# Nine raw weight buffers in the expert units, and six more for each small unit's first round

## The chip, the cores and the metric

One core of one Trainium2 chip runs the whole program. The metric is the device time of one execution in microseconds (us). Engines: PE (TensorE, matmuls), PEld (its weight loads), DVE (VectorE), ACT (ScalarE), POOL (GpSimd) and SP (SyncE, which here only issues DMAs).

## What is computed

A decoder trunk of two layers on 272 tokens (16 learned meta tokens and 256 real ones) of width 1024. Layer 0: stick-breaking attention and a dense SwiGLU. Layer 1: differential attention and a top-2-of-8 mixture of experts. The change touches the mixture alone:

```
logits = x @ w_router;  top_v, top_i = top_k(logits, 2);  gates = softmax(top_v)
for e in range(8):
    out += combine[:, e] * ((silu(x @ w_gate[e]) * (x @ w_up[e])) @ w_down[e])
```

Everything is float32. An expert has three matrices of 1024 x 3584 (gate, up, and down turned round), together 44 MB; all eight are read from the chip's memory once, 352 MB in 336 pieces.

## The kernel before

**Units.** The experts are taken as eight units, in the order wide, wide, small, wide, small, wide, small, wide. A wide unit holds up to 128 tokens, a small one up to 64; the experts are sorted by their number of tokens so that they fit. More wide units can follow if the tokens are spread unevenly.

**Pieces.** A unit's weights come as PIECES = 42 pieces of 128 x 2048 float32 (1 MB). For each of FC = 7 groups of 512 hidden columns there are two pieces of gate, two of up and two of down. Piece 0 is the first. SP issues one DMA per piece, in order, into one of RAW_SLOTS = 7 raw buffers (six quarters of `raw` and one `raw_more`), piece p into buffer p mod 7.

**A wide unit** multiplies in split form, to keep float32 precision at TensorE's faster rate: ACT copies a piece to `wh` (high half, line 880), DVE subtracts to get `wl` (low half, line 1427), and PE multiplies high x high, high x low and low x high (lines 2235, 2236, 2241 for gate and up, 2259, 2260, 2267 for down). `wh` and `wl` each have SPLIT_SLOTS = 3 places of a piece. A raw buffer is free when DVE has made the low half (`wl_ready`). A place of `wh` or `wl` is free when PE has read it (`wh_used`, `w_used`).

**A small unit** multiplies the raw float32 pieces directly, gate and up side by side in the two column halves of the array (lines 2360, 2362), down likewise in two halves (line 2391). It uses neither `wh` nor `wl`. A raw buffer is free when PE has multiplied with it (`few_used`, which rises by 2 after a pair of gate and up pieces).

**What SP waits for.** Before piece p SP waits until the piece 7 places earlier in the stream has freed its buffer: in a wide unit `wl_ready`, in a small one `few_used`, and for the first seven of a unit the count of the unit before. SP's waits are in order: while it waits for one buffer it issues nothing behind. The loop over the three pairs (small unit, wide unit) is a `Fori`; it reads each unit's expert number with a `value_load` ahead of each of its two units.

**Around it.** At the end of a wide unit ACT copies the 128 x 1024 output to `y`, and POOL stores it (512 KB, line 617) and then fetches the rows of the unit after the next (line 609); their DMAs run on POOL's queue, through the same 16 DMA engines.

Of the kernel before, what the change touches and what calls it, by code (L numbers as in the profile page):

```python
# [27 lines left out]
F32R = mybir.dt.float32r  # L28
# [6 lines left out]
P = 128  # L35
# [10 lines left out]
E = 8  # L46
# [6 lines left out]
CHUNK = 4096  # L53
# [40 lines left out]

RAW_SLOTS, SPLIT_SLOTS = 7, 3
MAX_UNITS = E + 4
# [87 lines left out]
def build(nc, tokens, vectors, sb_qkv, sb_o, d_qkv, d_o, ffn_gate, ffn_up, ffn_down, router, moe_gate, moe_up, moe_down, final_norm,  # L184
          c_base, c_stick, c_diff, c_route, c_zero, out):
    ctx = ExitStack()
    with ctx:
# [9 lines left out]
        raw = sb("raw", [P, 3, CHUNK])  # L197
        wh = sb("wh", [P, 2, CHUNK], F32R)
        wl = sb("wl", [P, 2, CHUNK], F32R)

        hT = sb("hT", [P, KD, L])
# [63 lines left out]
        def experts(own):  # L265
# [12 lines left out]
            return b  # L278

        xh, xl = phase(parts)  # L280
        sq3, raw_more = phase(lambda own: (sb("sq3", [P, 4 * BANK], where=own), sb("raw_more", [P, PIECE], where=own)))
# [10 lines left out]
        raw_landed = [sem(f"raw_landed{i}") for i in range(3)]  # L292
        piece_landed = [sem(f"piece_landed{i}") for i in range(RAW_SLOTS)]
        wh_ready, wl_ready = sem("wh_ready"), sem("wl_ready")
# [91 lines left out]
        for i in range(FC):  # L386
            for half in range(2):
                few_pieces[few_up_at(i) + 2 * half] = ("g", i, half)
                few_pieces[few_up_at(i) + 2 * half + 1] = ("u", i, half)
                few_pieces[few_down_at(i) + half] = ("d", i, half)  # L390

        def raw_piece(p):

            slot = p % RAW_SLOTS
            if slot == RAW_SLOTS - 1:
                return raw_more[:]
            return raw[:, slot // 2, slot % 2 * PIECE:(slot % 2 + 1) * PIECE]

# [8 lines left out]

        def piece_in(u, p):

            return u * (16 * PIECES // RAW_SLOTS) + 16 * (p // RAW_SLOTS + 1)  # L410

# [30 lines left out]
        def _(sp):  # L442
# [25 lines left out]

            def load_piece(e, p, kind, i, half):

                source = weights_of[kind][bass.ds(e * (FC * 2 * P) + P * (2 * i + half), P), :]
                sp.dma_start(raw_piece(p), source).then_inc(piece_landed[p % RAW_SLOTS], 16)

            def load_first():
                for p in range(PIECES):
                    kind, i = unit_chunks[p // 2]
                    if p < RAW_SLOTS:

                        sp.wait_ge(wl_ready, max(c for c in range(C_MOE) if c % 3 == min(p // 2, 2)) + 1 if p < 6 else C_MOE)
                    else:  # L480
                        sp.wait_ge(wl_ready, C_MOE + p + 1 - RAW_SLOTS)
                    load_piece(0, p, kind, i, p % 2)

            def load_wide(a, e, few_before):

                for p in range(PIECES):
                    kind, i = unit_chunks[p // 2]
                    if few_before is not None and p < RAW_SLOTS:
                        sp.wait_ge(few_used, few_before * PIECES + PIECES + p + 1 - RAW_SLOTS)
                    else:  # L490
                        sp.wait_ge(wl_ready, a * PIECES + C_MOE + p + 1 - RAW_SLOTS)
                    load_piece(e, p, kind, i, p % 2)

            def load_few(v, e):

                for p, (kind, i, half) in enumerate(few_pieces):
                    if p < RAW_SLOTS:
                        sp.wait_ge(wl_ready, (v + 1) * PIECES + C_MOE + p + 1 - RAW_SLOTS)
                    else:
                        sp.wait_ge(few_used, v * PIECES + p + 1 - RAW_SLOTS)  # L500
                    load_piece(e, p, kind, i, half)

            load_first()
            sp.wait_ge(routed, 1)
            load_wide(1, sp.value_load(bm["unit_i"][0:1, 1:2], min_val=0, max_val=E - 1), None)
            with sp.Fori(1, len(SMALL_UNITS) + 1) as v:
                load_few(v, sp.value_load(bm["unit_i"][0:1, bass.ds(2 * v, 1)], min_val=0, max_val=E - 1))
                load_wide(v + 1, sp.value_load(bm["unit_i"][0:1, bass.ds(2 * v + 1, 1)], min_val=0, max_val=E - 1), v)

            wides = sp.value_load(bm["unit_i"][0:1, 15:16], min_val=WIDE_UNITS, max_val=MAX_UNITS - len(SMALL_UNITS))  # L510
            with sp.If(wides > WIDE_UNITS):
                with sp.Fori(WIDE_UNITS, wides) as a:
                    e = sp.value_load(bm["unit_i"][0:1, bass.ds(a + len(SMALL_UNITS), 1)], min_val=0, max_val=E - 1)
                    load_wide(a, e, None)

# [114 lines left out]
        def _(act):  # L630
# [242 lines left out]

            def unit_split(u, a, p, first=False):

                act.wait_ge(piece_landed[p % RAW_SLOTS], piece_in(u, p))

                act.wait_ge(wh_used, split_free(a, p, first))
                act.wait_ge(wl_ready, split_free(a, p, first))
                act.copy(split_piece(wh, p), raw_piece(p)).then_inc(wh_ready, 1)  # L880
# [89 lines left out]

            def unit_body(u, a, scatter, first=False, few_next=False):

# [5 lines left out]
                for j, (kind, i) in enumerate(unit_chunks):  # L978
                    if 2 * j + 3 < PIECES:
                        unit_split(u, a, 2 * j + 3)  # L980
                    if kind == "d" and i + 1 < FC:
                        turned_high(i + 1)
                    if 2 * j + 4 < PIECES:
                        unit_split(u, a, 2 * j + 4)
                    if (kind, i) == ("g", 1):
# [20 lines left out]

            unit_body(0, 0, False, first=True)
            unit_split(1, 1, 0)
            unit_split(1, 1, 1)
            output_out(1, 1)  # L1010
            unit_split(1, 1, 2)
            with act.Fori(1, len(SMALL_UNITS) + 1) as v:
                unit_body(2 * v - 1, v, False, few_next=True)
                output_out(2 * v, v + 1)
                few_body(v)
                unit_split(2 * v + 1, v + 1, 0)
                unit_split(2 * v + 1, v + 1, 1)
                few_out(v)
                unit_split(2 * v + 1, v + 1, 2)

# [10 lines left out]
            wides = act.value_load(bm["unit_i"][0:1, 15:16], min_val=WIDE_UNITS, max_val=MAX_UNITS - len(SMALL_UNITS))  # L1031
            unit_body(STORED, WIDE_UNITS - 1, True)
            with act.If(wides > WIDE_UNITS):
                for n in range(2 * QT):
                    scale_for_more(n)
                with act.Fori(WIDE_UNITS, wides) as a:
                    u = a + len(SMALL_UNITS)
                    last_outputs(u, a)
                    unit_split(u, a, 0)
                    unit_split(u, a, 1)  # L1040
                    unit_split(u, a, 2)
                    gathered_high(a + 1)
                    unit_body(u, a, True)

# [671 lines left out]
        def _(pe):  # L1716
# [628 lines left out]
            def few_body(v):  # L2345

                def up(i, half):

                    p = few_up_at(i) + 2 * half
                    out_, few = ps[:, i % 2, :], bm["few"]  # L2350
                    pe.wait_ge(piece_landed[p % RAW_SLOTS], piece_in(2 * v, p))
                    pe.wait_ge(piece_landed[(p + 1) % RAW_SLOTS], piece_in(2 * v, p + 1))
                    if half == 0 and i >= 2:

                        pe.wait_ge(few_prod, (v - 1) * FC + i - 1)
                    for k in range(KD // 2):
                        to = slice((half * (KD // 2) + k) * SMALL, (half * (KD // 2) + k + 1) * SMALL)
                        s = slice(k * WIDE, (k + 1) * WIDE)
                        first_, last_ = half == 0 and k == 0, half == 1 and k == KD // 2 - 1
                        g = pe.matmul(out_[0:SMALL, :], few[:, to], raw_piece(p)[:, s], start=first_, stop=last_,  # L2360
                                      skip_group_check=True)
                        u = pe.matmul(out_[SMALL:, :], few[:, to], raw_piece(p + 1)[:, s], start=first_, stop=last_,  # L2362
                                      skip_group_check=True)
                    g.then_inc(few_used, 1)
                    u.then_inc(few_used, 1)
# [11 lines left out]
                def down(i, half):  # L2377

                    p = few_down_at(i) + half
                    if half == 0:  # L2380
                        pe.wait_ge(few_act_ready, (v - 1) * FC + i + 1)
                        if i == 0:

                            pe.wait_ge(y_ev, 4 * v + 2)
                    pe.wait_ge(piece_landed[p % RAW_SLOTS], piece_in(2 * v, p))
                    for k in range(2):
                        to = slice((half * 2 + k) * SMALL, (half * 2 + k + 1) * SMALL)
                        first_, last_ = i == 0 and half == 0 and k == 0, i == FC - 1 and half == 1 and k == 1
                        for h in range(2):
                            s = slice(k * D + h * BANK, k * D + (h + 1) * BANK)  # L2390
                            ins = pe.matmul(ps[h * SMALL:(h + 1) * SMALL, 2, :], bm["few_act"][:, i % 2, to], raw_piece(p)[:, s],
                                            start=first_, stop=last_, skip_group_check=True)
# [93 lines left out]
```

## Time and profile before

| | us |
|---|---|
| median of 3 runs (1406.06 to 1407.02) | 1406.73 |
| the profiled execution | 1405.3 |
| its span | 1403.5 |

| engine | busy us | share |
|---|---|---|
| PE | 1325.2 | 94% |
| DVE | 875.6 | 62% |
| ACT | 724.1 | 52% |
| POOL | 69.6 | 5% |
| SP's DMA queue | 422.67 MB | 76.4% of 16 DMA engines' time |

The busy share is an average over stages. A matmul counts as busy also while it is stretched or waits inside the engine, so a high share doesn't mean that PE does all it can. The mixture of experts fills the last two thirds of the span. The granted clock of TensorE was 0.985 of its full speed on average.

### The profile page before, as it was taken

To read this page: it belongs to the slowest core of one execution; us is meant where nothing else is said; L and a number is where in the kernel's file an instruction comes from. 1 tells how busy PE (TensorE), PEld (TensorE's weight loads), DVE (VectorE), ACT (ScalarE), POOL (GpSimd) and SP (SyncE) were. 2 spreads that over 40 slices of the span, in tenths; PEclk is the share of its full clock that TensorE was granted. 3 is DMA by queue.
4 is the path that set the end of the run, shared out by engine and by line. 5 is a ranking of instruction groups with operands and counts; after the bars stand their busy time and mean duration, and the time that the engine had idled before them with its cause. 6 is when DMAs were issued, how large, how long until landed. Compare 5 with 4: busy or idle time off the path is not lost.

```text
span 1403.5 us, 19596 instructions
## 1 busy us (share of the span) xinstructions
PE 1325.2 (94%) x7528; PEld 1031.4 (73%) x7528; DVE 875.6 (62%) x954; ACT 724.1 (52%) x719; POOL 69.6 (5%) x92
## 2 busy tenths in 40 slices
PE   9999999999999999999997889998779998888997
PEld 8999999999999778888852258872238884226786
DVE  6554766544987699988830168860128881017897
ACT  7564544344566777777720057750027771006775
POOL 0100000000000063000000000000000000002000
PEclk9999999999999999999999999999999999999999
DMA  8563553553442799999989999989999999999992
GB/s 315 194 224 120 180 180 121 193 183 108 175 166 69 276 343 380 421 407 406 372 317 421 421 407 421 416 339 387 421 420 407 421 359 356 421 421 420 421 421 105
DMA packets 75877, 440.55 MB, mean 314 GB/s; under 512 B 7296, under 2 KB 9344, under 8 KB 30672
## 3 DMA queue, kind: packets, MB, share of 16 engines
q1 hardware_dynamic: 71680, 422.67, 76.4%
q0 software_dynamic: 3952, 16.49, 3.3%
q8 instruction: 66, 1.08, 0.3%
q14 instruction: 35, 0.29, 0.1%
q10 hardware_dynamic: 144, 0.02, 0.0%
HBM read 433.12 MB, written 11.01 MB: 316 GB/s over the span
## 4 chain that ended last, share of the span: by engine, by line
PE 72%; DMA 13%; DVE 7%; issue 4%; ACT 3%; SPq 0%; DVEq 0%; ACTq 0%
PE ps L2235 9%; PE ps L2236 9%; PE ps L2241 8%; DMA raw<-in_moe_w_gate 8%; PE ps L2360 7%; PE ps L1740 4%; PE ps L2259 4%; PE ps L2267 4%; PE ps L2260 4%; PE ps L1730 4%; PE ps L1731 4%; DMA raw<-in_moe_w_up 3%; PE ps L1778 2%; PE ps L1795 2%; PE ps L1779 2%
## 5 line engine op out<-in xcount | busy, mean ns | idle before, releaser
L1427 DVE TENSOR_TENSOR wl<-raw,wh 128x2048 fp32r<-128x2048 f32 x180 | 410.9, 2290 | 62.5 <-ACT wh L880 61.5
L880 ACT CAST wh<-raw 128x2048 fp32r<-128x2048 f32 x180 | 344.3, 1914 | 144.7 <-PE ps L2236 57.2
L2235 PE MATMUL ps<-wh,gh 128*128 128x512 f32 x560 | 222.0, 396 | 11.5 <-issue 8.4
L2236 PE MATMUL ps<-wh,gl 128*128 128x512 f32 x560 | 220.6, 394 | 0.0
L2360 PE MATMUL ps<-raw,few 128*64 128x512 f32 x288 | 139.3, 633 | 37.1 <-issue 28.7
L2362 PE MATMUL ps<-raw,few 128*64 128x512 f32 x312 | 155.8, 650 | 0.0
L2241 PE MATMUL ps<-wl,gh 128*128 128x512 f32 x560 | 151.3, 392 | 0.2 <-DVE wl L1427 0.2
L944 ACT ACTIVATE sil<-ps 64x512 f32<-64x512 f32 x21 | 12.4, 588 | 261.6 <-PE ps L2362 261.6
L2235 PEld LDWEIGHTS ps<-wh,gh 128*128 128x128 f32 x560 | 106.2, 190 | 37.3 <-issue 13.5
L2360 PEld LDWEIGHTS ps<-raw,few 128*64 128x64 f32 x288 | 39.2, 145 | 120.0 <-issue 120.0
L2236 PEld LDWEIGHTS ps<-wh,gl 128*128 128x128 f32 x560 | 106.2, 190 | 23.0
L2241 PEld LDWEIGHTS ps<-wl,gh 128*128 128x128 f32 x560 | 105.3, 188 | 23.9 <-DVE wl L1427 0.7
L1091 DVE TENSOR_TENSOR wl<-raw,wh 128x4096 fp32r<-128x4096 f32 (+1 forms) x18 | 73.2, 4069 | 61.8 <-ACT wh L639 39.7
L639 ACT CAST wh<-raw 128x4096 fp32r<-128x4096 f32 (+2 forms) x29 | 92.0, 3174 | 34.9 <-PE ps L1731 34.3
L2259 PE MATMUL ps<-wh,eah 128*128 128x512 f32 x272 | 109.2, 401 | 0.0
L1618 DVE COPY few_act<-ps 128x256 f32<-128x256 f32 x21 | 8.9, 425 | 159.6 <-PE ps L2374 159.6
L2260 PE MATMUL ps<-wh,eal 128*128 128x512 f32 x272 | 106.5, 391 | 0.0
L1730 PE MATMUL ps<-xh,wh 128*128 128x272 f32 x352 | 88.5, 288 | 0.2 <-DVE xl L1098 0.2
L1731 PE MATMUL ps<-xl,wh 128*128 128x272 f32 x352 | 88.3, 286 | 0.0
L1614 DVE TENSOR_TENSOR act<-sil,ps 64x512 f32<-64x512 f32 x21 | 14.5, 691 | 108.4 <-ACT sil L944 108.4
L2267 PE MATMUL ps<-wl,eah 128*128 128x512 f32 x272 | 73.4, 392 | 0.0
L1427 DVE TENSOR_TENSOR wl<-raw_more,wh 128x2048 fp32r<-128x2048 f32 x30 | 68.6, 2288 | 4.7 <-ACT wh L880 4.6
(353 smaller groups left out, 2378.2 us busy)
## 6 DMA issues: line engine op xcount, KB each, us to landing
raw<-in_moe_w_gate SPq DMA_DIRECT2D x101, 1024.0 KB, 11.3
raw<-in_moe_w_up SPq DMA_DIRECT2D x99, 1024.0 KB, 10.6
raw<-in_moe_w_down SPq DMA_DIRECT2D x88, 1024.0 KB, 12.1
raw_more<-in_moe_w_down SPq DMA_DIRECT2D x24, 1024.0 KB, 10.7
raw_more<-in_moe_w_up SPq DMA_DIRECT2D x13, 1024.0 KB, 14.1
raw<-in_diff_w_qkv SPq DMA_DIRECT2D x8, 1536.0 KB, 6.1
raw_more<-in_moe_w_gate SPq DMA_DIRECT2D x11, 1024.0 KB, 7.3
raw<-in_sb_w_qkv SPq DMA_DIRECT2D x7, 1536.0 KB, 7.7
```

The lines of the kernel that those rows point to most:

```text
L880: act.copy(split_piece(wh, p), raw_piece(p)).then_inc(wh_ready, 1)
L1427: dve.tensor_tensor(split_piece(wl, p), raw_piece(p), raw_f(split_piece(wh, p)), ALU.subtract).then_inc(wl_ready, 1)
L1730: pe.matmul(outp(m), w, highs(k), start=first and k == 0, stop=False, skip_group_check=True)
L1731: ins = pe.matmul(outp(m), w, lows(k), start=False, stop=False, skip_group_check=True)
L2235: pe.matmul(ps[:, bank, :], gh[:, s], w, start=(k0 + k == 0), stop=False)
L2236: ins = pe.matmul(ps[:, bank, :], gl[:, s], w, start=False, stop=False)
L2241: ins = pe.matmul(ps[:, bank, :], gh[:, s], low[:, k * WIDE:(k + 1) * WIDE], start=False, stop=(k0 + k == KD - 1))
L2259: pe.matmul(ps[:, 2 + h, :], ah[:, s], w, start=(i == 0 and k0 + k == 0), stop=False)
L2260: ins = pe.matmul(ps[:, 2 + h, :], al[:, s], w, start=False, stop=False)
L2267: ins = pe.matmul(ps[:, 2 + h, :], ah[:, s], w, start=False, stop=(i == FC - 1 and k0 + k == 3))
L2360: g = pe.matmul(out_[0:SMALL, :], few[:, to], raw_piece(p)[:, s], start=first_, stop=last_, skip_group_check=True)
L2362: u = pe.matmul(out_[SMALL:, :], few[:, to], raw_piece(p + 1)[:, s], start=first_, stop=last_, skip_group_check=True)
```

## The change

There are now RAW_SLOTS = 9 raw buffers for all expert units. The two new ones are the fourth quarters of `wh` and `wl`, which three split places leave unused in the expert stage. Beside them a small unit has LENT = 6 further buffers in its first round: the three places of `wh` and the three of `wl`, which the wide unit before it leaves as it ends.

The modulo rule gives way to two tables. WIDE_PLACES takes 42 pieces in rounds of 9, 8, 9, 8 and 8, so that each unit uses each buffer a fixed number of times; piece 41 of a wide unit follows piece 33 in its buffer instead of piece 34, and pieces 0 to 7 of a small unit follow pieces 34 to 41 of the wide one (before, pieces 0 to 6 followed 35 to 41). Piece 8 of a small unit goes where piece 25 was. FEW_PLACES takes the small unit's pieces in rounds of 15, 9, 9 and 9. Pieces 9 to 14 wait until PE has read pieces 39, 40 and 41 of the wide unit in high form (`wh_used`) or in low form (`w_used`). Piece 15 waits for piece 0, and from there on each waits for the one 9 earlier in its round.

At the very start of the mixture, pieces 7 and 8 of the first unit wait for the end of the attention's output projection (`w_used` at C_MOE) instead of for the first two low halves.

In SP's loop both `value_load`s now stand ahead of the small unit's loads. The counts that ACT and PE wait for are written with two factors (wide units and small units so far) instead of one. Multiplications, splits and all other work stay as they are. The core of the diff:

```diff
-RAW_SLOTS, SPLIT_SLOTS = 7, 3
+RAW_SLOTS, SPLIT_SLOTS = 9, 3
+LENT = 2 * SPLIT_SLOTS
+
+def places(rounds):
+    return [(s, n) for n, r in enumerate(rounds) for s in r]
+
+WIDE_PLACES = places((range(9), range(8), range(9), range(8), range(8)))
+FEW_PLACES = places((range(RAW_SLOTS + LENT), range(9), range(9), range(9)))
...
+        def raw_place(s):
+            if s < 6:
+                return raw[:, s // 2, s % 2 * PIECE:(s % 2 + 1) * PIECE]
+            if s == 6:
+                return raw_more[:]
+            part_, slot = (s - 7, SPLIT_SLOTS) if s < RAW_SLOTS else ((s - RAW_SLOTS) % 2, (s - RAW_SLOTS) // 2)
+            return unsplit[:, part_, slot // 2, slot % 2 * PIECE:(slot % 2 + 1) * PIECE]
...
+        def landed_by(a, few, taken, p):
+            s = taken[p][0]
+            wide_times, few_times = (sum(1 for at_ in t if at_[0] == s) for t in (WIDE_PLACES, FEW_PLACES))
+            return 16 * (wide_times * a + few_times * few + sum(1 for at_ in taken[:p + 1] if at_[0] == s))
...
+            def load_wide(a, e, few=None, first=False):
+                for p, (s, n) in enumerate(WIDE_PLACES):
+                    kind, i = unit_chunks[p // 2]
+                    if n:
+                        sp.wait_ge(wl_ready, a * PIECES + C_MOE + last_at(WIDE_PLACES[:p], s) + 1)
+                    elif first and s < 6:
+                        sp.wait_ge(wl_ready, max(c for c in range(C_MOE) if c % 3 == min(p // 2, 2)) + 1)
+                    elif first:
+                        sp.wait_ge(wl_ready if s == 6 else w_used, C_MOE)
+                    elif few is None:
+                        sp.wait_ge(wl_ready, a * PIECES + C_MOE - PIECES + last_at(WIDE_PLACES, s) + 1)
                     else:
+                        sp.wait_ge(few_used, few * PIECES + last_at(FEW_PLACES, s) + 1)
+                    load_piece(e, raw_piece(p), s, kind, i, p % 2)
+
+            def load_few(v, e):
+                for p, (kind, i, half) in enumerate(few_pieces):
+                    s, n = FEW_PLACES[p]
+                    if n:
+                        sp.wait_ge(few_used, v * PIECES + last_at(FEW_PLACES[:p], s) + 1)
+                    elif s < RAW_SLOTS:
+                        sp.wait_ge(wl_ready, v * PIECES + C_MOE + last_at(WIDE_PLACES, s) + 1)
                     else:
+                        lent = s - RAW_SLOTS
+                        sp.wait_ge((wh_used, w_used)[lent % 2], (v + 1) * PIECES + C_MOE + lent // 2 + 1 - SPLIT_SLOTS)
+                    load_piece(e, few_piece(p), s, kind, i, half)
...
             with sp.Fori(1, len(SMALL_UNITS) + 1) as v:
-                load_few(v, sp.value_load(bm["unit_i"][0:1, bass.ds(2 * v, 1)], min_val=0, max_val=E - 1))
-                load_wide(v + 1, sp.value_load(bm["unit_i"][0:1, bass.ds(2 * v + 1, 1)], min_val=0, max_val=E - 1), v)
+                few_e = sp.value_load(bm["unit_i"][0:1, bass.ds(2 * v, 1)], min_val=0, max_val=E - 1)
+                next_e = sp.value_load(bm["unit_i"][0:1, bass.ds(2 * v + 1, 1)], min_val=0, max_val=E - 1)
+                load_few(v, few_e)
+                load_wide(v + 1, next_e, few=v)
```

## Rows read from the trace of the kernel before

**Rows 1.** The page's second part: moved GB/s in 40 slices of the span.
```profile
GB/s 315 194 224 120 180 180 121 193 183 108 175 166 69 276 343 380 421 407 406 372 317 421 421 407 421 416 339 387 421 420 407 421 359 356 421 421 420 421 421 105
```

**Rows 2.** Windows: us, busy per engine, then granted clock, DMA share, GB/s.
```profile
590.00:697.00 107.00, 107.00 (x484) 87.97 (x483) 95.19 (x56) 80.61 (x55) 2.74 (x5) 1.00 1.01 399
...
717.00:722.00 5.00, 5.00 (x25) 1.91 (x25) 0.00 (x0) 1.07 (x2) 0.57 (x1) 1.00 0.45 181
722.00:727.00 5.00, 5.00 (x26) 1.65 (x24) 0.69 (x1) 0.59 (x1) 2.18 (x4) 1.00 0.91 314
727.00:740.00 13.00, 9.21 (x44) 2.75 (x40) 1.12 (x2) 0.59 (x1) 0.00 (x0) 1.00 1.01 350
740.00:816.00 76.00, 62.73 (x270) 22.00 (x272) 8.61 (x15) 4.01 (x7) 0.00 (x0) 0.93 1.01 421
```

**Rows 3.** Timeline of SP, the DMA issues at the first small unit's start.
```profile
713.83 0.33 SPq L472 DMA_DIRECT2D raw_more<-in_moe_w_gate  x1
721.54 0.33 SPq L472 DMA_DIRECT2D raw<-in_moe_w_up  x1
```

**Rows 4.** DMA issues in short windows at three unit changes; last column: us to landing.
```profile
raw_more<-in_moe_w_gate SPq DMA_DIRECT2D x1, 1024.0 KB, 4.9
raw<-in_moe_w_up SPq DMA_DIRECT2D x1, 1024.0 KB, 5.8
...
raw<-in_moe_w_gate SPq DMA_DIRECT2D x1, 1024.0 KB, 4.7
raw<-in_moe_w_up SPq DMA_DIRECT2D x1, 1024.0 KB, 5.0
...
raw<-in_moe_w_gate SPq DMA_DIRECT2D x1, 1024.0 KB, 4.9
raw<-in_moe_w_up SPq DMA_DIRECT2D x1, 1024.0 KB, 5.7
```

**Rows 5.** Chain of waits, 715 to 860: start us, us, what.
```profile
750.16 3.46 PE ps L2391 x16
753.79 15.20 DMA raw<-in_moe_w_gate
...
808.08 10.68 DMA raw<-in_moe_w_gate
818.91 1.91 ACT wh L880
```

**Rows 6.** Timeline of SP at the two later small units' starts and one end.
```profile
918.06 0.33 SPq L472 DMA_DIRECT2D raw_more<-in_moe_w_down  x1
925.09 0.34 SPq L472 DMA_DIRECT2D raw<-in_moe_w_gate  x1
925.63 0.33 SPq L472 DMA_DIRECT2D raw<-in_moe_w_up  x1
...
946.62 0.33 SPq L472 DMA_DIRECT2D raw<-in_moe_w_up  x1
...
1031.44 0.33 SPq L472 DMA_DIRECT2D raw_more<-in_moe_w_down  x1
1032.75 0.34 SPq L472 DMA_DIRECT2D raw<-in_moe_w_gate  x1
...
1149.74 0.34 SPq L472 DMA_DIRECT2D raw<-in_moe_w_gate  x1
...
1171.50 0.33 SPq L472 DMA_DIRECT2D raw<-in_moe_w_up  x1
```

**Rows 7.** Timeline of DVE, two low halves near the second small unit.
```profile
912.94 2.29 DVE L1427 TENSOR_TENSOR wl<-raw,wh 128x2048 fp32r<-128x2048 f32 x1 [0.45 <-ACT wh L880]
915.75 2.29 DVE L1427 TENSOR_TENSOR wl<-raw_more,wh 128x2048 fp32r<-128x2048 f32 x1
```

**Rows 8.** Timeline of POOL at the first small unit's start.
```profile
719.34 0.57 POOL L617 DMA_DIRECT2D output_slots<-y  x1 [107.64 <-ACT y L953]
```

**Rows 9.** Windows: one whole period, small unit and wide unit.
```profile
717.90:942.90 225.00, 203.79 (x897) 126.72 (x896) 114.75 (x76) 94.27 (x70) 5.98 (x11) 0.97 0.98 397
```

More of the change, by code:

```diff
@@ L278, in experts, with splits @@
             return b
+        def splits(own):
+            return sb("wh", [P, 2, CHUNK], F32R, where=own), sb("wl", [P, 2, CHUNK], F32R, where=own)
+        wh, wl = phase(splits)
+        unsplit = phase(lambda own: sb("unsplit", [P, 2, 2, CHUNK], where=own))
+        sb("splits", [P, 4 * CHUNK])
         xh, xl = phase(parts)
@@ L292, in build @@
         raw_landed = [sem(f"raw_landed{i}") for i in range(3)]
-        piece_landed = [sem(f"piece_landed{i}") for i in range(RAW_SLOTS)]
+        piece_landed = [sem(f"piece_landed{i}") for i in range(RAW_SLOTS + LENT)]
         wh_ready, wl_ready = sem("wh_ready"), sem("wl_ready")
@@ L390, in build, with few_piece, last_at @@
                 few_pieces[few_down_at(i) + half] = ("d", i, half)
-        def raw_piece(p):
[L394 to L397, printed above, removed]
+        def raw_place(s):
[5 more added lines that the diff above has]
+            return unsplit[:, part_, slot // 2, slot % 2 * PIECE:(slot % 2 + 1) * PIECE]
+        def raw_piece(p):
+            return raw_place(WIDE_PLACES[p][0])
+        def few_piece(p):
+            return raw_place(FEW_PLACES[p][0])
+        def last_at(taken, s):
+            return max([p for p, at_ in enumerate(taken) if at_[0] == s], default=None)
         def half_of(parts_, i):
@@ L467, in _, with load_piece @@
                 sp.dma_start(dst, src).then_inc(raw_landed[c % 3], 16)
-            def load_piece(e, p, kind, i, half):
+            def load_piece(e, to, s, kind, i, half):
                 source = weights_of[kind][bass.ds(e * (FC * 2 * P) + P * (2 * i + half), P), :]
-                sp.dma_start(raw_piece(p), source).then_inc(piece_landed[p % RAW_SLOTS], 16)
-            def load_first():
-                for p in range(PIECES):
+                sp.dma_start(to, source).then_inc(piece_landed[s], 16)
@@ L872, in square_tokens, with unit_split @@
                                accum_out=small[:, 10 + n:11 + n]).then_inc(tok_squared, 1)
[L874 to L876 removed]
+            def unit_split(few, a, p, first=False):
+                act.wait_ge(*wide_in(a, few, p))
                 act.wait_ge(wh_used, split_free(a, p, first))
@@ L969, in scale_for_more, with unit_body @@
                 act.mul(part_, part_, rsT[:, n % 2:n % 2 + 1]).then_inc(tok_scaled, 1)
-            def unit_body(u, a, scatter, first=False, few_next=False):
+            def unit_body(u, few, a, scatter, first=False, few_next=False):
                 def turned_high(i):
```

73 lines of the change are left out of this document (28 added, 45 removed).

## The prediction

> **What bounds the kernel now.** I read the page's second part first. In the mixture of experts (slice 14 on) most slices move 420 GB/s or a little less, and nothing in the kernel moves more than 421: the DMA engines are full there, with dents [rows 1]. The windows say where each side is the bound. Inside a wide unit PE has no idle time at all (107.0 of 107.0 us) and the queue keeps pace at 399 GB/s. Inside a small unit the DMA moves 421 GB/s at a full share while PE has gaps (62.7 of 76 us) [rows 2]. So a wide unit is PE's, a small unit is the queue's. A small unit ends when its last piece has landed, and the next wide unit starts right behind it: its first piece is issued at 808.08, lands 10.68 us later, and ACT's split starts at 818.91, within 0.2 us [rows 5]. What a small unit costs is therefore the number of pieces not yet landed when PE enters it, at the queue's pace, plus any time in which the queue stands empty.
>
> The pace: 1 MB is 1.0486 MB in decimal, at 421 GB/s [rows 2] 2.49 us. PE's need in a small unit: 3.46 us for two pieces of down [rows 5], and for the first pair of gate and up from 717.9 (the start of the unit, the left edge of [rows 9]) to the issue that waits for it at 721.54 [rows 3], about 3.6 us. That is 1.75 us a piece, and 74 us for 42 pieces. PE has room against 42 x 2.49 = 104.6 us.
>
> The queue does stand empty, at one place: the start of each small unit. From 717 to 722 the DMA share is 0.45, from 722 to 727 it is 0.91, and then it is full [rows 2]. SP issues piece 6 at 713.83 and piece 7 only at 721.54 [rows 3]. All seven buffers are taken, and the eighth load has to wait until PE has multiplied with the first pair. The two later units show the same: piece 7 at 946.62 and at 1171.50 [rows 6].
>
> **The change part by part.**
>
> (1) More buffers at the start of a small unit. Piece 7 now follows piece 41 of the wide unit and waits for its low half, as piece 6 does now, so it goes out at 713.83. Piece 8 is free at once, pieces 9 to 14 wait for PE to have read pieces 39 to 41. The last of these reads ends with the wide unit at 717.9, and piece 15 waits for the first pair at 721.5. By then seven further loads of 2.49 us lie in the queue. It can't run dry, and the whole rest of the unit (PE needs less than the queue brings) and the first pieces of the next wide unit shift with piece 7's landing. So I compare that one landing.
>
> First small unit: now 721.54 + 5.8 = 727.3 [rows 3, 4]. After: 713.83 + 4.9 = 718.7, by what piece 6 took. Gain 8.6.
>
> Second and third: here piece 0 is late. SP issues the wide unit's last piece at 918.06, and the loop's turn takes until 925.09 (7.0 us) before piece 0 goes out [rows 6]. After the change piece 41 waits for piece 33 instead of 34, which DVE finishes at 912.94 + 2.29 = 915.23 instead of 915.75 + 2.29 = 918.04 [rows 7], 2.8 us earlier. The second `value_load` now also stands at the head of the loop. Its price is the step from 1031.44 to 1032.75 (1.31 us, with a `value_load` between) less that from 925.09 to 925.63 (0.54 us) [rows 6], 0.77 us. Piece 0 so goes out at 925.09 - 2.81 + 0.77 = 923.05 and lands 4.7 later [rows 4], at 927.8. Seven more pieces at 2.49 bring piece 7 to 945.2. Now it is 946.62 + 5.0 = 951.6 [rows 4, 6]. Gain 6.4. Third: 1149.74 - 2.04 + 4.9 + 17.4 = 1170.0 against 1171.50 + 5.7 = 1177.2, gain 7.2. Sum of the three: 22.2 us.
>
> (2) What filled the gap. POOL stores the wide unit's output at 719.34 [rows 8], 0.5 MB in decimal, 1.25 us at 421 GB/s. Today it runs while the weights' queue is empty; afterwards it takes time from the pieces. The bounds are 0 and 1.25 us per unit; I take 1.25, three times, 3.75 us. The fetch behind it falls into a nearly full queue now already (0.91 and 1.01 [rows 2]) and stays as it is.
>
> [...] No row here shows the store beside a full queue.
>
> (3) The pair of new buffers inside the wide units. PE is never idle there, so a longer lead buys nothing inside. It is also no cost: SP's loads are issued one or two pieces earlier and otherwise in the same order. The first unit's pieces 7 and 8 go out before the first splits; the queue is idle there anyway. Zero, with a bound of one piece (2.5 us) in either direction.
>
> (4) Wait counts with two factors, on ACT and PE. A register step is not shown by itself. SP's whole step between two issues, with its wait's count, is 0.54 us of which 0.33 is the issue [rows 6], so a count costs at most 0.2 us; ACT's wide-unit piece has 2.8 us (the pitch of [rows 7]) for a copy of 1.91 [rows 5], and PE in a small unit has over 0.7 us per piece. Covered: zero. Without that cover 0.1 us on 210 + 126 pieces would be some 30 us, but no row hints at it.
>
> (5) The granted clock of PE is 0.93 in the small unit's window and 1.00 in the others [rows 2]. A shorter small unit has fewer gaps. I take zero; either way it is hidden, because the landing decides the unit's end.
>
> Sum: 22.2 - 3.75 = 18.4 us. The profiled execution takes 1405.3 with a span of 1403.5; after, 1386.9. Against the median of the runs, which is 1.4 us longer, 1388.3.
>
> **What is the most it could be.** One period (small and wide unit) is 225.0 us at a mean of 397 GB/s [rows 9]: 89.3 MB, which at 421 are 212.2 us. So at most 12.8 us per period can go, of which the unit starts explain 6.4 to 8.6; part of the rest is the lower rate of POOL's transfers at a full share (350 GB/s from 727 to 740 [rows 2]).
>
> **The rivals.**
>
> A: half the lead is lost. The lent buffers bring nothing, say because the queue takes no more loads at once than it has held, so that piece 9 still comes after the first pair. Then pieces 7 and 8 alone are ahead: 2 x 2.49 = 5.0 us per unit at most, 15 in sum, less the store's 3.75, 11.2 us; 1395.5. For it: no more than six loads (15.2 us from issue to landing [rows 5]) ever were in the queue. Against it: two or three in the queue are enough to bridge the gap of 7.7 us.
>
> B: nothing moves. The queue is the bound over the whole period and the gap reappears elsewhere, say at the loop's turn in SP or behind the next small unit. Price: the gain falls to 0 to 3 us, 1405. Against it: the loads ahead of a small unit are issued at DVE's pitch of 2.8 us [rows 7], slower than the queue's 2.49, so a gap that closes is not owed later.
>
> C: slower. The deeper queue lowers the rate for the weights, as in the window of 727 to 740, where the share is 1.01 and only 350 GB/s pass [rows 2], 3.0 us per piece. Place: the 34 pieces from piece 8 to the end of a small unit. Price at that rate: 34 x 0.5 = 17 us per unit, less the gain of 6.1, 11 us slower each, 33 in all, 1439. It decides from 6.1 / 34 = 0.18 us per piece on, that is below 393 GB/s. For it only that window, which holds POOL's small transfers; against it the 421 GB/s with six pieces queued. [...]
>
> D: more. The loop's turn is shorter or overlaps, and the ahead-running queue closes both the 2 us left at piece 0 of the second and third unit and the store's share: 22 to 27 us, 1382.
>
> **How the numbers follow.** Forecast (16 to 21 us) 0.62, A with all between 5 and 16 us 0.18, B 0.05, C 0.04, D 0.11. The predicted time is 1388.3. The range has to leave out no more than two in ten: it takes in D down to a gain of 25.7 (1381), and A up to 9 us (1398); B, C and the edges of A and D are outside. About 0.2% (2.8 us) is what a measurement of this kernel can tell from no change. Faster by more than that: the forecast, A, D and a third of B, 0.93. Within: 0.03. Slower: 0.04.
>
> **What would show it.** Step 1: SP's piece 7 right behind the wide unit's last low half (about 7.7 us earlier to the first small unit), a DMA share near 1 from 717 to 727, and a first small unit of about 94 us in place of 101 (717.9 to 818.9). Step 1b: piece 0 of the second and third small unit 7.0 + 0.8 us behind the wide unit's last piece, and a short gap in the queue still there. Step 2: GB/s of the weights dips where POOL stores. Step 3 and 4: the wide units keep their length (the second from 818.9 [rows 5] to the right edge of [rows 9], 124 us). The prediction is wrong if PE shows gaps at the end of small units that no landing explains (then PE or ACT has become the bound), if the rate in small units falls below 421, or if wide units grow.

## The result and the profile after

The changed kernel takes 1398.07 us (median of 4 runs, 1396.48 to 1399.20) against 1406.51 us of the kernel before beside it: a ratio of 0.9937, 95% interval 0.9922 to 0.9952. It is 8.4 us faster. The forecast was 18.4 us faster, 1388.3 us, and the range ended at 1398.0. The direction was right, the forecast gain was more than double the measured one. The profiled execution took 1398.2 us with a span of 1395.9.

The first view is the page's first part of the changed kernel. The work is the same, and PE is busy a little longer (1327.8 us, before 1325.2) in a shorter span:

```profile
PE 1327.8 (95%) x7528; PEld 1032.8 (74%) x7528; DVE 875.6 (63%) x954; ACT 723.0 (52%) x719; POOL 69.7 (5%) x92
```

The gap of [rows 3] is closed. This is SP's timeline of the changed kernel at the first small unit (start us, us, what) and at the turn of its loop ahead of the second:

```profile
713.89 0.33 SPq L510 DMA_DIRECT2D raw_more<-in_moe_w_gate  x1
717.61 0.33 SPq L510 DMA_DIRECT2D unsplit<-in_moe_w_up  x1
718.12 0.88 SPq L510 DMA_DIRECT2D unsplit<-in_moe_w_down  x2
...
914.48 0.33 SPq L510 DMA_DIRECT2D unsplit<-in_moe_w_down  x1
921.89 0.34 SPq L510 DMA_DIRECT2D raw<-in_moe_w_gate  x1
```

Piece 7 is issued 3.7 us behind piece 6, no longer 7.7, and pieces 8 and 9 follow at once. The turn of the loop took 7.4 us, where 7.8 were expected. The windows of the changed kernel (as [rows 2] and [rows 9]):

```profile
717.00:722.00 5.00, 5.00 (x24) 3.80 (x24) 0.58 (x1) 0.00 (x0) 0.00 (x0) 1.00 0.88 320
722.00:727.00 5.00, 5.00 (x24) 1.68 (x26) 0.00 (x0) 1.07 (x2) 0.57 (x1) 1.00 1.02 400
727.00:740.00 13.00, 13.00 (x64) 4.50 (x62) 1.81 (x3) 1.18 (x2) 2.19 (x4) 1.00 1.02 378
...
721.90:942.60 220.70, 204.00 (x897) 126.79 (x896) 114.77 (x76) 94.17 (x70) 6.00 (x11) 0.98 1.00 405
```

The DMA share from 717 on is 0.88, then 1.02, in place of 0.45 and 0.91. The period is 220.7 us, in place of 225.0. That is 4.3 us, where the working had 7.35 for the first. So where are the missing ones? The next view tells: the small units' multiplications with raw pieces, in windows that end at 800, 1000 and 1200 us, before each unit does (count, shortest/median/longest ns, first and last start us). Kernel before:

```profile
L2360 PE MATMUL ps<-raw,few x88: 592/592/1085, 717.9 to 794.6; 128*64 128x512 f32 x88
L2360 PE MATMUL ps<-raw,few x64: 592/592/1061, 942.9 to 999.1; 128*64 128x512 f32 x64
L2360 PE MATMUL ps<-raw,few x40: 592/592/1061, 1167.8 to 1199.7; 128*64 128x512 f32 x40
```

Changed kernel:

```profile
L2402 PE MATMUL ps<-raw,few x58: 592/592/679, 721.9 to 799.7; 128*64 128x512 f32 x58
L2402 PE MATMUL ps<-raw,few x47: 592/592/643, 942.6 to 999.7; 128*64 128x512 f32 x47
L2402 PE MATMUL ps<-raw,few x31: 592/592/643, 1164.6 to 1199.8; 128*64 128x512 f32 x31
```

The first small unit begins at 721.9 instead of 717.9: 4.0 us were lost before the change could gain anything. Most of them fall in the two wide units ahead of it, in which PE is busy almost without a pause in both kernels (199.5 and 199.7 of the 200 us from 500 to 700). The small units themselves take 94.5, 95.7 and 95.2 us (from their first to their last matmul), before 100.7, 100.2 and 100.4: 15.9 us gained. The wide units are longer. From the first expert matmul to the first small unit, which are two wide units, it is 241.3 us in place of 238.2, which is 3.1 of the 4.0; the rest is a later first expert matmul (480.6 in place of 479.6). The three stretches behind the small units (a wide unit each, the last with the kernel's end) add 1.8, 1.7 and 0.9 us. So 15.9 gained, 7.5 lost in wide units and 1.0 at the start leave the 7.6 us by which the span is shorter (1403.5 to 1395.9), but for rounding.

The reason is in PE's timeline. These are the starts of two groups of four low-half matmuls of gate and up, three pieces or 36 matmuls apart, first in the kernel before, then in the changed one:

```profile
646.40 1.08 PE L2241 MATMUL ps<-wl,gh 128*128 128x512 f32 x4
...
654.64 1.08 PE L2241 MATMUL ps<-wl,gh 128*128 128x512 f32 x4
```

```profile
649.37 1.08 PE L2283 MATMUL ps<-wl,gh 128*128 128x512 f32 x4
...
657.74 1.09 PE L2283 MATMUL ps<-wl,gh 128*128 128x512 f32 x4
```

8.24 us against 8.37: a matmul of 512 columns is followed by the next after 229 ns before, after 232.5 ns now. I took the mean of all such steps in a trace (some 2450 each, from the starts in the timeline): 228.6 to 229.4 ns in the kernel before, 232.3 to 233.0 in the changed one, in every line alike (high with high, high with low, low with high). The granted clock is 1.00 in both stretches. 3.5 ns on 210 pieces of 12 matmuls are 8.8 us. PE's own work had become slower, which my sum had at zero.

### The profile page after: what moved, and what is told of

It reads as the page before. It is cut to its first block, busy times and chain, and to the rows that moved or that the text cites. A ratio compares the mean times of both kernels' runs of the same rounds, so it can differ in the third digit from the quotient of the medians.

```text
span 1395.9 us, 19602 instructions
## 1 busy us (share of the span) xinstructions
PE 1327.8 (95%) x7528; PEld 1032.8 (74%) x7528; DVE 875.6 (63%) x954; ACT 723.0 (52%) x719; POOL 69.7 (5%) x92
## 4 chain that ended last, share of the span: by engine, by line
PE 76%; DMA 16%; DVE 4%; ACT 2%; issue 1%; SPq 0%; DVEq 0%; ACTq 0%
PE ps L2277 9%; PE ps L2278 9%; PE ps L2283 8%; DMA unsplit<-in_moe_w_up 8%; PE ps L2402 6%; DMA raw<-in_moe_w_gate 5%; PE ps L1782 4%; PE ps L2301 4%; PE ps L2309 4%; PE ps L2302 4%; PE ps L1772 4%; PE ps L1773 4%; PE ps L1820 2%; PE ps L1821 2%; PE ps L1837 2%; DMA raw_more<-in_moe_w_down 2%
## 5 line engine op out<-in xcount | busy, mean ns | idle before, releaser
L1469 DVE TENSOR_TENSOR wl<-raw,wh 128x2048 fp32r<-128x2048 f32 x150 | 342.5, 2289 | 61.7 <-ACT wh L922 61.0
L922 ACT CAST wh<-raw 128x2048 fp32r<-128x2048 f32 x150 | 285.9, 1907 | 126.4 <-PE ps L2278 56.6
L2402 PE MATMUL ps<-raw,few 128*64 128x512 f32 x216 | 101.9, 621 | 26.3 <-issue 23.3
L2404 PE MATMUL ps<-raw,few 128*64 128x512 f32 x216 | 102.3, 623 | 0.0
L2402 PEld LDWEIGHTS ps<-raw,few 128*64 128x64 f32 x216 | 29.0, 142 | 87.6 <-issue 87.6
L1469 DVE TENSOR_TENSOR wl<-unsplit,wh 128x2048 fp32r<-128x2048 f32 x35 | 80.1, 2287 | 6.6 <-ACT wh L922 6.6
L922 ACT CAST wh<-unsplit 128x2048 fp32r<-128x2048 f32 x35 | 66.9, 1913 | 28.5 <-PE ps L2278 11.7
```

Source lines behind the costliest of these rows:

```text
L1469: dve.tensor_tensor(split_piece(wl, p), raw_piece(p), raw_f(split_piece(wh, p)), ALU.subtract).then_inc(wl_ready, 1)
L2402: g = pe.matmul(out_[0:SMALL, :], few[:, to], few_piece(p)[:, s], start=first_, stop=last_, skip_group_check=True)
L2404: u = pe.matmul(out_[SMALL:, :], few[:, to], few_piece(p + 1)[:, s], start=first_, stop=last_, skip_group_check=True)
```

## The experiments

**What could slow PE.** The diff doesn't touch a matmul of the wide units. It does three other things to them: it moves `wh` and `wl` in SBUF (they are now allocated behind the small tiles, not behind `raw`), it lets DMAs land in parts of `wh` and `wl`, and it changes the wait counts. In the compiled program `wh` has gone from byte 65664 to 88256 of each partition, while `gh` stays at 190528. `wl`, `gl`, `eah` and `eal` lie whole multiples of 2048 bytes from these.

**Moving the tiles alone.** In the changed kernel:

```diff
         wr = sb("wr", [P, KD, E])
...
+        sb("pad_low", [P, 16])
         wh, wl = phase(splits)
         unsplit = phase(lambda own: sb("unsplit", [P, 2, 2, CHUNK], where=own))
         sb("splits", [P, 4 * CHUNK])
+        sb("pad_high", [P, 16])
```

> The changed kernel with 64 bytes of padding per partition ahead of wh and wl and 64 behind them: both tiles lie 64 bytes higher, everything behind them 128 bytes higher, all else is the same. Theory P (place): in the changed kernel PE's step from one 512-column matmul to the next in the wide units is 232.5 ns instead of 229 because wh and wl have moved from an address that is a multiple of 128 bytes to one that is not (88256 = 689.5 x 128). It expects the step back at 229 ns, the wide units 1.6 to 1.9 us shorter each, and the time at 1398.1 - 9 = 1389 us. Rival T (traffic): the wide units are slower because DMAs now land in wh and wl while PE reads them. Rival W (wait counts): the counts with two factors cost time. Both expect no change: 232.5 ns and 1398 us.

Measured: 1388.94 us (1388.51 to 1392.06), ratio 0.9880 (0.9864 to 0.9896), steps of 228.3 to 229.5 ns. The padding gave back 9.1 us against 1398.07, or 7.7 against a_shift_all below (1396.66), which was timed beside it and has the changed kernel's steps. DMAs still land in `wh` and `wl` and the counts still have two factors, so T and W are refuted. This kernel is the forecast's kernel: with PE's work as before, its time is 0.6 us from the forecast of 1388.3. Beside its own runs of the kernel before (1407.04) it gains 18.1 us by the medians and 16.9 by the ratio. Its small units:

```profile
L2404 PE MATMUL ps<-raw,few x64: 592/592/1057, 718.0 to 799.0; 128*64 128x512 f32 x64
L2404 PE MATMUL ps<-raw,few x50: 592/592/1087, 935.7 to 999.8; 128*64 128x512 f32 x50
L2404 PE MATMUL ps<-raw,few x40: 592/592/643, 1156.3 to 1197.9; 128*64 128x512 f32 x40
```

The first begins at 718.0, as before. Periods of 217.7 and 220.6 us, and from the third small unit's start to the end of the span 230.3 (1386.6 - 1156.3), where the kernel before has 225.0, 224.9 and 235.7: gains of 7.3, 4.3 and 5.4 us. My sum had 7.35, 5.15 and 5.95.

The other two runs are one with the same padding in the kernel before, and one with the lower padding alone in the changed one:

> The kernel before with the same 64 bytes ahead of wh and wl and 64 behind them, nothing else. Theory P: the step between 512-column matmuls rises from 229 to 232.5 ns and the time from 1406.5 by about 9 to 1415 us. Rivals T and W: nothing changes, 1406.5 us, since no DMA lands in wh or wl in the expert units here and no count has two factors.

> The changed kernel with the 64 bytes ahead of wh and wl alone, so that also the stationary operands of the wide units (gh, gl, eah, eal) and xh, raw_more and all behind lie 64 bytes higher, now at multiples of 128 bytes. If only the place of the moving operand counts, 1389 us as with both paddings. If the place of the stationary operand counts too, the step falls below 229 ns and the time below 1389 us by up to some us. Rivals T and W: 1398 us.

Measured: b_shift64 1403.89 us (1402.38 to 1405.91), ratio 0.9977 (0.9968 to 0.9986), steps of 227 ns for gate and up. It became faster, where theory P had it 9 us slower. a_shift_all 1396.66 us (1394.31 to 1397.80), ratio 0.9931 (0.9917 to 0.9944), steps of 231.9 to 233.1 ns, though `wh`, `gh` and the rest are all at multiples of 128 there. P falls with both. What orders all five kernels is the distance from the moving operand to the stationary one, so I formed theory D.

**The distance.** `wh` and `wl` stay where the changed kernel has them, and only what lies behind moves:

```diff
         sb("splits", [P, 4 * CHUNK])
+        sb("pad_high", [P, 32])      # 128 bytes; 48 for 192, 96 for 384
```

> The changed kernel with 128 bytes of padding per partition behind wh and wl: wh and wl stay at the changed kernel's address (88256), all behind them, gh, gl, eah and eal among it, lies 128 bytes higher. The five kernels so far have steps between 512-column matmuls that go with the distance from the moving operand (wh, wl) to the stationary one (gh, gl, eah, eal), modulo 512 bytes: 0 gives 227.0 ns (b_shift64), -64 gives 229.1 (before, a_shift64), -128 gives 232.5 (changed, a_shift_all). Theory D (distance): here the distance is 0, so 227 ns and 1398.1 - 210 pieces x 12 matmuls x 5.5 ns = 1384 us. Rival P (the address of wh and wl alone, a multiple of 128 or not): as the changed kernel, 232.5 ns and 1398 us.

> The changed kernel with 192 bytes behind wh and wl: distance +64 modulo 512. Theory D: not the 232.5 ns of the changed kernel; if the cost depends on the size of the offset alone, 229 ns as at -64 and about 1389 us. Rival P: 232.5 ns and 1398 us.

> The changed kernel with 384 bytes behind wh and wl: distance +256 modulo 512, the farthest. Theory D: if the cost grows with the offset, 232.5 ns or more, 1398 us or more; if it repeats every 256 bytes, 227 ns and 1384 us. Rival P: 232.5 ns.

Measured: c_gap128 1388.49 us (1387.32 to 1389.05), ratio 0.9859 (0.9842 to 0.9875); c_gap192 1399.1 us and c_gap384 1385.8 us, one run each. PE's timeline of c_gap128, three pieces apart as above:

```profile
645.49 1.07 PE L2284 MATMUL ps<-wl,gh 128*128 128x512 f32 x4
...
653.65 1.07 PE L2284 MATMUL ps<-wl,gh 128*128 128x512 f32 x4
```

and of c_gap192:

```profile
649.73 1.09 PE L2284 MATMUL ps<-wl,gh 128*128 128x512 f32 x4
...
658.13 1.09 PE L2284 MATMUL ps<-wl,gh 128*128 128x512 f32 x4
```

8.16 us (226.7 ns a step) against 8.40 (233.3). D's order holds: 256 bytes count like 0, so the distance works modulo 256. Two sizes were off. +64 isn't like -64 but the worst of all (233.3), and the time of c_gap128 is 1388.5, not 1384. c_gap128 has the first small unit at 716.4, 1.6 us ahead of a_shift64, and then small units of 95.0, 96.1 and 95.7 us in place of 93.4, 95.0 and 95.1. My reading is a giving back that I had left out: a small unit ends by the queue, and a faster wide unit leaves the queue less time to run ahead. The traces bear it out for the second and third small unit, where piece 7 lands 3.7 and 2.9 us behind the unit's start in place of 2.6 and 2.1. They don't for the first, where it lands after 0.7 us in both. Those 1.6 us stay open, and e_gap384 below, also at distance 0, has 94.2 there.

The same two operands, told apart inside one kernel: 128 bytes ahead of `gh` and 128 more ahead of `eah`, which brings gate and up to distance 0 and leaves down at 128 modulo 256.

> The changed kernel with 128 bytes of padding ahead of gh and 128 more ahead of eah: the distance from wh and wl to gh and gl becomes 0 modulo 256, the distance to eah and eal stays at 128 modulo 256 as in the changed kernel. wh and wl don't move. Theory D (the distance of the two operands of a matmul, modulo 256): within one kernel, the gate and up matmuls (with gh, gl) step at 227.0 ns and the down matmuls (with eah, eal) at 232.5 ns; the time is between the two, about 1391 us. If the place of something else counts (the whole block behind wl, or the DMAs), all have one step.

```profile
647.19 1.07 PE L2283 MATMUL ps<-wl,gh 128*128 128x512 f32 x4
...
655.35 1.08 PE L2283 MATMUL ps<-wl,gh 128*128 128x512 f32 x4
658.13 1.10 PE L2309 MATMUL ps<-wl,eah 128*128 128x512 f32 x4
```

Gate and up: 8.16 us for three pieces, 227.0 to 227.4 ns over the whole trace; down: 232.3 to 233.4 ns. 1392.9 us (one run). So it is the pair of operands that counts, not the DMAs nor the block as a whole.

**The loss put into the kernel before.** Nothing but padding behind its `wl`:

```diff
         wl = sb("wl", [P, 2, CHUNK], F32R)
+        sb("pad_high", [P, 48])      # 192 bytes; 16 for 64
```

> The kernel before with 192 bytes of padding behind wh and wl and nothing else: the distance from wh to gh is 128 modulo 256, as in the changed kernel. Theory D: steps of 232.5 ns; the first two wide units take 84 x 12 x 3.5 ns = 3.5 us longer, the later ones 1.8 us each, of which the small units give back a part, because the queue goes on while PE is slow: 1407.5 + 5 to 9 = 1412 to 1417 us. If the loss of the changed kernel came from its new buffers or counts, this one stays at 1407.5.

> The kernel before with 64 bytes behind wh and wl: distance 0 modulo 256 with wh and wl at their old address. Theory D: 227 ns and 1403.9 us as b_shift64 (1402.4 to 1405.9). If the address of wh and wl mattered beside the distance, it would differ from b_shift64.

```profile
648.52 1.08 PE L2242 MATMUL ps<-wl,gh 128*128 128x512 f32 x4
...
656.88 1.09 PE L2242 MATMUL ps<-wl,gh 128*128 128x512 f32 x4
```

Measured: f_before_gap192 1415.00 us (1412.68 to 1416.59), ratio 1.0054 (1.0038 to 1.0071), steps of 232.3 to 233.2 ns; f_before_gap64 1403.71 us (1402.27 to 1405.03), ratio 0.9975 (0.9966 to 0.9985), the same as b_shift64, whose `wh` lies 64 bytes higher. So 192 bytes of nothing cost the old kernel 7.8 us (from 1407.21 beside it), and the address of `wh` doesn't count beside the distance. All of it in one table (steps of gate and up, ns; ratios to the kernel before):

| distance modulo 256 | step | old buffers | new buffers |
|---|---|---|---|
| 0 | 227.0 | 0.9975 | 0.9859 |
| 192 | 229 | 1 | 0.9880 |
| 128 | 232.5 | 1.0054 | 0.9937 |
| 64 | 233.3 | not run | 1399.1 us, one run |

Down each column the padding changes the time; across each row the new buffers do, by a factor of 0.9884, 0.9880 and 0.9884. The other new kernels at these distances (a_shift_all with 0.9931 at 128, e_gap384 below with 0.9868 at 0) give 0.9878 and 0.9893. At a like distance the new buffers are worth 1.1 to 1.2%, 15 to 17 us, at each of the three distances.

The first two wide units, before any small one, show the distance cleanly in all the kernels. From the first expert matmul to the first small unit it is 236.7 or 236.8 us at distance 0, 238.2 at 192, 241.3 at 128 and 242.1 at 64, with old and with new buffers alike; d_split, with one distance for gate and up and another for down, has 238.1.

**Which buffers carry the gain.** The changed kernel with both paddings and no lent buffers:

```diff
-LENT = 2 * SPLIT_SLOTS
+LENT = 0
...
-FEW_PLACES = places((range(RAW_SLOTS + LENT), range(9), range(9), range(9)))
+FEW_PLACES = places((range(9), range(9), range(9), range(9), range(6)))
```

> The changed kernel with both paddings and without the six lent buffers: LENT = 0, a small unit in rounds of 9, 9, 9, 9 and 6. Piece 9 of a small unit then waits for the first pair. The sum of the prediction says: piece 8 is the last ahead, the queue runs dry after it for 7.7 - 2 x 2.5 = 2.7 us in the first small unit and less in the others, so this kernel is 3 to 8 us slower than the one with both paddings: 1392 to 1397 us by theory P, 1401 to 1406 by T and W.

SP's timeline, first small unit:

```profile
714.37 0.33 SPq L512 DMA_DIRECT2D unsplit<-in_moe_w_down  x1
721.70 0.33 SPq L512 DMA_DIRECT2D raw<-in_moe_w_down  x1
```

These are piece 8 and, after a wait of 7.3 us for the first pair, piece 9. 1393.32 us (1392.92 to 1393.74), ratio 0.9905 (0.9890 to 0.9920): 4.4 us behind a_shift64, inside the 3 to 8 expected. The two raw buffers alone gain 13.7 us, so the six lent ones add a quarter of the gain.

The reverse, seven raw buffers and the six lent, 384 bytes of padding:

> The changed kernel with 384 bytes behind wh and wl, seven raw buffers in rounds of 7 as before, and the six lent buffers for a small unit's first round. Piece 6 is then followed at once by pieces 7 to 12, which wait only for reads that end with the wide unit. The sum's view: piece 7 comes 3.6 us later than with nine (it waits for the read of piece 39 behind piece 41's low half, not one place earlier), the queue doesn't run dry afterwards. So 2.5 us per small unit are lost against e_gap384, some 3 to 8 us in all: 1389 to 1394 us. If the two extra raw buffers carried the gain alone, it would be 1398 us or more.

It took 1414.22 us (1411.26 to 1415.04), ratio 1.0041 (1.0027 to 1.0056): slower than the kernel before. That is far above the 1389 to 1394 us expected. The other reading (1398 or more) fits it only by the number, since a kernel without any new buffer takes 1403.7 us at this distance. The trace shows why, and the fault is in my table of rounds (13, 7, 7, 7, 7 and 1). This is SP at the end of the second small unit:

```profile
1028.08 0.34 SPq L511 DMA_DIRECT2D raw<-in_moe_w_down  x1
1041.66 0.92 SPq L511 DMA_DIRECT2D raw<-in_moe_w_gate  x2
```

Piece 41 sat alone in the last round, in buffer 0, which the next unit's piece 0 needs. SP waits in order, so no load of the next unit went out for 13.6 us, until the small unit was over. Mended by a round that holds only buffer 6 behind the first:

```diff
-FEW_PLACES = places((range(RAW_SLOTS + LENT), range(7), range(7), range(7), range(7), range(1)))
+FEW_PLACES = places((range(RAW_SLOTS + LENT), (6,), range(7), range(7), range(7), range(7)))
```

> As e_lent_only (seven raw buffers, six lent, 384 bytes of padding), with the small unit's rounds arranged so that its last seven pieces are in buffers 0 to 6 in order; in e_lent_only piece 41 sat in buffer 0, and the next wide unit's first load waited for it, until the small unit was over. Expected: the next wide unit's loads go out ahead again, and the time is 2.5 us per small unit less the share given back above e_gap384 (1389.1): 1390 to 1396 us. If lent buffers without more raw ones are worth nothing, about 1404 us, as the kernel before at this distance.

1397.02 us (1396.03 to 1398.91), ratio 0.9930 (0.9914 to 0.9947). That is 6.7 us below the kernel before at the same distance (1403.7), and 1 us above the range that I expected. Against c_gap128 the small units are 1.6, 2.2 and 2.8 us longer, about the one piece of 2.5 us that goes out later. The lent buffers alone are worth 6.7 us, the raw ones alone 13.7, both 15 to 18: the two overlap. That either bridges part of the same gap is how I read it; no run separates the overlap further.

**The turn of SP's loop.** Written out, on top of the padding of 128 and of 384:

> As c_gap128, and SP's loop over the three pairs of units is written out, so that there is no turn of a loop ahead of the second and third small unit. The prediction's sum left about 2.4 us of empty queue there. If the 7 us from the wide unit's last issue to piece 0 are the loop's turn, they fall to some 2 us, and the time falls by 2 x 2.4 = 4.8 us at most against c_gap128. If they are the value_loads and waits, nothing changes.

```profile
911.69 0.33 SPq L511 DMA_DIRECT2D unsplit<-in_moe_w_down  x1
914.65 0.33 SPq L511 DMA_DIRECT2D raw<-in_moe_w_gate  x1
```

The step fell from 7.4 to 3.0 us, so it was the loop's turn. Its time, 1387.35 us (1385.46 to 1393.82), ratio 0.9852 (0.9836 to 0.9869), can't be told from c_gap128. Repeated on 384 bytes beside the plain kernel:

> The same program as c_gap384, timed in rounds: distance 0 modulo 256. Theory D: the same as c_gap128, 1388.5 us (1387 to 1389). If the one run of 1385.8 us was typical, something beyond the distance modulo 256 is better by 2 to 3 us.

> e_gap384 with SP's loop written out. In c_unrolled the step from the wide unit's last issue to piece 0 fell from 7.4 to 3.0 us, but the time only by 1.1 us. Expected again: 0 to 2 us below e_gap384, because the queue has work for most of that gap now.

1389.11 us (1388.51 to 1389.88), ratio 0.9868 (0.9852 to 0.9885), and 1388.64 us (1385.11 to 1390.00), ratio 0.9862 (0.9843 to 0.9881). The single 1385.8 of c_gap384 wasn't typical, and 384 is no better than 128. Writing the loop out is worth nothing that these runs can tell. The version to keep is c_gap128: the change, with 128 bytes of padding, 1388.5 us, 1.4% faster than the kernel before. These runs don't tell it from e_gap384 (0.9868) or surely from a_shift64 (0.9880); the intervals overlap.

## Why the prediction was right and wrong

**The bound, and where the gap is: right.** Units that are PE's and units that are the queue's, and an empty queue at each small unit's start; the share there rose as told, and the changed kernel's small units are 15.9 us shorter in sum.

**Step 1, three landings of piece 7: right.** Piece 7 was to be issued 4.1 us ahead of the small unit's start (713.83 against 717.9). It goes out 4.3 us ahead in the changed kernel (717.61 against 721.9). The turn of the loop came out as worked out, within 0.4 us. The landings are best seen in a_shift64, where PE's pace is as before. Piece 7 of the three small units, its issue and the us to its landing:

```profile
713.85 0.33 SPq L512 DMA_DIRECT2D unsplit<-in_moe_w_up  x1
unsplit<-in_moe_w_up SPq DMA_DIRECT2D x1, 1024.0 KB, 4.8
...
931.60 0.33 SPq L512 DMA_DIRECT2D unsplit<-in_moe_w_up  x1
unsplit<-in_moe_w_up SPq DMA_DIRECT2D x1, 1024.0 KB, 6.7
...
1152.12 0.33 SPq L512 DMA_DIRECT2D unsplit<-in_moe_w_up  x1
unsplit<-in_moe_w_up SPq DMA_DIRECT2D x1, 1024.0 KB, 6.3
```

The first lands at 718.7, as forecast. Counted from each unit's start (718.0, 935.7, 1156.3) they land after 0.7, 2.6 and 2.1 us, where the working had 0.8, 2.3 and 2.2. The kernel before has 9.4, 8.7 and 9.4, so the landings come 22.1 us earlier in sum, against 22.2 forecast.

**Step 2, POOL's store at its upper bound: held within the sum.** Steps 1 and 2 together were 18.4 us; a_shift64 shows 16.9 us of span and 18.1 us of median. Its small units are 7.3, 5.2 and 5.3 us shorter, 17.8 in sum, against 7.35, 5.15 and 5.95. So 4.3 of the 22.1 us of earlier landings are lost again inside the small units, where the store was put at 3.75. That it would be the upper bound was my estimate; no row of the kernel before shows the store beside a full queue. The last 0.9 us between 17.8 and 16.9 is a second wide unit behind a small one of 125.5 us in place of 124.6, which stays open. The store itself is seen beside the full queue in the changed kernel. Before, POOL issued it at 719.34 and then its fetch, which waits until the store has landed, at 723.83:

```profile
723.83 2.18 POOL L609 DMA_DIRECT2D xn<-token_slots  x4 [3.92 <-DMA output_slots<-y]
```

In the changed kernel, with a load of SP issued ahead of the store and its us to landing:

```profile
722.00 0.33 SPq L510 DMA_DIRECT2D unsplit<-in_moe_w_down  x1
unsplit<-in_moe_w_down SPq DMA_DIRECT2D x1, 1024.0 KB, 24.6
...
723.38 0.57 POOL L659 DMA_DIRECT2D output_slots<-y  x1 [109.31 <-ACT y L995]
732.75 2.19 POOL L651 DMA_DIRECT2D xn<-token_slots  x4 [8.80 <-DMA output_slots<-y]
```

The store now takes up to 9.4 us from its issue to its landing, before up to 4.5. But it doesn't wait for the load issued ahead of it, which lands only at 746.6. So it isn't served in order of issue. It takes its time from the weights: the two loads that land meanwhile come 4.1 and 3.5 us apart in place of 2.5. That speaks for the upper of the two bounds or a little more, as the 4.3 us against 3.75 do.

**Step 3, zero for the wide units with 2.5 us either way: the step that failed.** It was argued from loads and waits alone. The same diff moves `wh` and `wl` by 22592 bytes, which changes the distance to the stationary operands from 192 to 128 modulo 256, and that costs 3.5 ns on each of 2520 matmuls. At this distance the new kernel is 9.1 us slower than with the padding of a_shift64 (1398.07 against 1388.94), nearly the whole miss of 9.8; against a_shift_all, timed beside a_shift64, it is 7.7. In the profile the first two wide units take 3.1 us longer than in a_shift64 (241.3 against 238.2), where 84 pieces of 12 steps make 3.5. The three periods behind are 3.0, 1.4 and 1.0 us longer, 5.4 in sum, where 126 pieces make 5.3. The later first expert matmul (480.6 instead of 479.6) has no part in this: it lies between 479.4 and 480.6 in all traces but one (482.1), and at 479.8 in a_shift_all and 479.7 in f_before_gap192, which have the changed kernel's distance. I had named the right sign for it ("if wide units grow"), but no mechanism and no price.

**Step 4, wait counts: right at zero.** They are in c_gap128, which steps at 227 ns. **Step 5, the clock in small units: covered, as said.** It is 0.94 to 0.96 there in the changed kernel, and PE still has gaps (59.9 busy of 76 us in the row below), and the landing decided the unit's end: the next wide unit's first piece, issued at 796.65, lands 19.92 us later, and ACT's split starts at 816.73.

**The rivals.** A had a time near the measured one (1395.5) but not its mechanism: piece 9 follows piece 8 at once in the changed kernel. The kernel without lent buffers is A's case, with a gain of 13.7 us where A had 11.2 at most. That the queue takes no more loads than it has held is refuted with C, the lower rate in a deeper queue. These are a load of the changed kernel's first small unit with its us to landing, and the window behind POOL's transfers (as [rows 2], 4 us later):

```profile
739.47 3.16 SPq L510 DMA_DIRECT2D unsplit<-in_moe_w_up  x1
unsplit<-in_moe_w_up SPq DMA_DIRECT2D x1, 1024.0 KB, 29.9
...
744.00:820.00 76.00, 59.89 (x261) 20.42 (x260) 9.87 (x16) 6.70 (x9) 0.00 (x0) 0.96 1.01 421
```

At 739.47 eleven loads are on their way, and the rate is 421 GB/s as before. (The kernel before already has a load of 18.2 us, issued at 1285.75, longer than the 15.2 us by which the prediction put the depth at six.) B is refuted by the small units' length. D, 22 us or more, is reached by no kernel that was timed more than once, and writing out the loop, D's mechanism, gains nothing that can be told.

## What to carry to other kernels

A diff that moves a tile can change the time of engines that it doesn't name (here PE's step, from 229 to 232.5 ns): where PE is the bound, compare the step between like matmuls before and after, before looking for a cause among the buffers, and try a few paddings. Buffers should be counted by what the queue has to bridge (here a wait of 7.7 us, or three loads); two plain ones alone did three quarters of it. In a table of rounds look at who sits in the buffer that the next unit needs first: one piece in the wrong place cost 17 us (1414.2 against 1397.0).

## What the runs showed of the hardware

In these kernels the pace of back-to-back matmuls with a moving operand of 128 x 512 fp32r depends on the distance in SBUF between moving and stationary operand, modulo 256 bytes: 227.0 ns at 0, 229 at 192, 232.5 at 128, 233.3 at 64, at a granted clock of 1.00. It doesn't depend on either address alone: it is 227.0 ns with `wh` at byte 65664, 65728 and 88256, and with `gh` at the same byte 190656 it is 227.0 in c_gap128 and 229 in a_shift64. With 272 columns, ahead of the experts, the differences are smaller. The steps are 123.6 to 126.1 ns by line, and one line's mean differs by 1.3 ns at most between kernels. A part of that does go with the layout (a line of the feed-forward with `ah` and `wl`: 124.8 ns in the kernels at distance 0, 125.0 in the kernel before, 125.6 in the changed one); it wasn't sorted by its own operands' distance. PE waits for no engine in these stretches (it is busy in 60.00 of the 60 us from 620 to 680 in the kernel before, the changed one, c_gap128 and c_gap192 alike), and still the distance between what it reads as moving and as stationary operand shifts the step by 2.8% (227.0 to 233.3 ns). Why it does, and why with a period of 256 bytes, no run tells.
